# A hybrid attention stage on one core: heads alternate between two kinds, with five items of lead instead of three

## The reference, cut to what matters

```python
def sb_attend(q_pos, q, k, v, k_pos):
    z = einsum('bhqd,bhkd->bhqk', q, k) * (HEAD_DIM ** -0.5)
    mask = k_pos[None, :] < q_pos[:, None]
    log_skip = where(mask, log_sigmoid(-z), 0.0)
    later = cumsum(log_skip, axis=3, reverse=True) - log_skip
    w = where(mask, exp(log_sigmoid(z) + later), 0.0)
    return einsum('bhqk,bhkd->bhqd', w, v)

def fox_attend(q_pos, q, fq, k, v, k_pos, fk):
    z = einsum('bhqd,bhkd->bhqk', q, k) * (HEAD_DIM ** -0.5)
    z = z + fq[..., :, None] - fk[..., None, :]
    z = where(k_pos[None, :] <= q_pos[:, None], z, -inf)
    return einsum('bhqk,bhkd->bhqd', softmax(z), v)
```

## Time and profile before

| what | value |
|---|---|
| median of 3 runs | 1671.12 us (1670.85 to 1672.43) |
| the profiled execution | 1671.85 us |
| its span in the profile | 1670.1 us |
| TensorE busy, share of the span | 1488.6 us, 89% |
| VectorE busy | 939.3 us, 56% |
| ScalarE busy | 755.8 us, 45% |
| mean granted TensorE clock | 0.951 |

### The profile page before, as it was taken

The page is one execution under the profiler, slowest core; times in us unless marked ns, Lnnn a source line. Parts: engine busy times, 40 slices in busy tenths (PEclk is TensorE's granted clock), DMA queues, the critical chain, the costliest instruction groups (busy, mean ns, idle before and its releaser), DMA issues. The chain is left out here.

```text
span 1670.1 us, 23300 instructions
## 1 busy us (share of the span) xinstructions
PE 1488.6 (89%) x8581; PEld 1318.0 (79%) x8581; DVE 939.3 (56%) x1189; ACT 755.8 (45%) x1079; POOL 181.5 (11%) x129
## 2 busy tenths in 40 slices
PE   5999999999999988888999989969955998999950
PEld 3689899999999977777899989958844876788840
DVE  7622012223324338888766635442246998999948
ACT  8622011223333327776666622131114876777823
POOL 0000000000000010000000001111103334334320
PEclk9999999999999989999999989979966999999975
DMA  8355444457666568575677433444316899999538
GB/s 294 91 154 184 131 133 140 149 166 220 197 208 206 186 178 206 156 187 128 148 176 180 103 102 123 155 166 142 116 50 218 254 337 291 277 280 280 102 52 325
DMA packets 233075, 300.10 MB, mean 180 GB/s; under 512 B 86441, under 2 KB 171537, under 8 KB 232954
## 3 DMA queue, kind: packets, MB, share of 16 engines
q1 hardware_dynamic: 223458, 264.01, 51.8%
q0 software_dynamic: 9504, 34.61, 8.7%
HBM read 264.23 MB, written 87.81 MB: 211 GB/s over the span
## 5 line engine op out<-in xcount | busy, mean ns | idle before, releaser
L745 PE MATMUL G<-hhi,proj_whi 128*128 128x384 f32 x768 | 178.7, 341 | 0.0
L745 PE MATMUL G<-hhi,proj_wlo 128*128 128x384 f32 x768 | 176.4, 338 | 0.0
L745 PE MATMUL G<-hlo,proj_whi 128*128 128x384 f32 x768 | 176.3, 338 | 0.0
L1995 DVE TENSOR_TENSOR experts_ulo<-plain,experts_uhi 128x2048 fp32r<-128x2048 f32 x66 | 151.1, 2290 | 16.6 <-ACT experts_uhi L1939 9.8
L1098 PE MATMUL G<-items_WT,items_vt 128*128 128x128 f32 x1152 | 151.7, 277 | 0.3 <-DMA items_vc<-in_cache_sb_v_dram 0.3
L1098 PEld LDWEIGHTS G<-items_WT,items_vt 128*128 128x128 f32 x1152 | 142.2, 192 | 1.1 <-DMA items_vc<-in_cache_sb_v_dram 0.5
L1939 ACT ACTIVATE experts_uhi<-plain 128x2048 fp32r x66 | 126.7, 1921 | 33.6 <-PEq L80 23.4
L745 PEld LDWEIGHTS G<-hhi,proj_whi 128*128 128x128 f32 x768 | 136.1, 188 | 2.7 <-DVE proj_wlo L825 2.2
L745 PEld LDWEIGHTS G<-hhi,proj_wlo 128*128 128x128 f32 x768 | 138.0, 188 | 0.0
L745 PEld LDWEIGHTS G<-hlo,proj_whi 128*128 128x128 f32 x768 | 137.9, 188 | 0.0
L1896 PE MATMUL G<-experts_uhi,experts_ghi 128*128 128x512 f32 x264 | 108.9, 412 | 8.3 <-DVE experts_glo L1999 7.0
(11 more groups left out here) (313 smaller groups left out, 3030.9 us busy)
## 6 DMA issues: line engine op xcount, KB each, us to landing
plain<-in_w_dram SPq DMA_DIRECT2D x132, 512.0 KB
plain<-in_w_dram SPq DMA_DIRECT2D x33, 1024.0 KB
proj_wraw<-in_w_ada_dram SPq DMA_DIRECT2D x32, 512.0 KB
proj_wraw<-in_w_in_dram SPq DMA_DIRECT2D x20, 512.0 KB
qkhi_d<-proj_ohi SPq DMA_DIRECT2D x16, 576.0 KB, 2.8
qklo_d<-proj_olo SPq DMA_DIRECT2D x16, 576.0 KB, 3.0
gate_d<-proj_full SPq DMA_DIRECT2D x16, 576.0 KB, 3.7
merge_sg<-gate_d SPq DMA_DIRECT2D x16, 576.0 KB, 6.4
```

Source lines behind the costliest of these rows:

```text
L745: m = pe.matmul(G[:, g + c, 0:CH], w[r][:, k, :], a[:, k, c * CH:(c + 1) * CH], start=k == 0 and q == 0, stop=k == KD - 1 and q == 2)
L1995: dve.tensor_tensor(half(ulo[j], c), raw_up(side[n], c), half(uhi[j], c).bitcast(F32), ALU.subtract).then_inc(u_lo, 1)
```

## The change

All of it is in stage_items:
- The heads alternate, SB head h and then FoX head h. q, k, kc, vt, vc and W2 have one buffer for each kind. F has one buffer (fb) instead of two.
- AHEAD becomes 5: six S buffers (with as many maxima and sums), four R buffers (RING). ScalarE's exponent and VectorE's stick and invert move to i+4, weigh, least and scores to i+5.
- The cached-key scores of a head are computed with item 1, in the bank that item 1 leaves free, and added up by VectorE (add_past) there; item 3's scores wait for this sum, and the late item transposes zt itself. turn_past goes.
- high_y copies y from PSUM into one of three buffers yt (y_taken), waits for this copy, and rounds from there into yhi. The y bank is free once the copy is made. low_y runs at i-4 (LATER) and reads yt instead of the bank.

```diff
-                AHEAD = 3
+                AHEAD = 5
+                RING = 4
-                fb = [sb(f"fb{j}", [P, SEQ + 2 * P]) for j in both]
+                fb = sb("fb", [P, SEQ + 2 * P])
-                R = [sb(f"R{i}", [P, SEQ]) for i in range(2)]
+                R = [sb(f"R{i}", [P, SEQ]) for i in range(RING)]
+                NY, LATER = 3, 4
+                yt = [sb(f"yt{i}", [P, 512]) for i in range(NY)]
-                heads = [(k // H, k % H) for k in range(2 * H)]
+                heads = [(k % 2, k // 2) for k in range(2 * H)]
...
                         if f:
-                            if h >= 2:
-                                sp.wait_ge(min_ready, TT * (h - 1))
-                            load_f(h)
-                        if k % 2 == 0 and k:
-                            if k >= 4:
-                                sp.wait_ge(pv_done, n_pv[TT * (k - 2)])
-                            load_v(k // 2)
+                            if h:
+                                sp.wait_ge(min_ready, TT * h)
...
+                        if h % 2 == 0 and k:
+                            if k >= 2:
+                                sp.wait_ge(pv_done, n_pv[TT * (k - 1)])
+                            load_v(f, h, u)
...
+                        if t == 1:
+                            pe.wait_ge(kc_in[f], KC_DMAS * (h + 1))
+                            for b in range(NB):
+                                new = slice(SEQ + b * NQ, SEQ + (b + 1) * NQ)
+                                m = pe.matmul(G[:, g + 1, b * 2 * NQ:(b + 1) * 2 * NQ], kc[f][:, b * PAST:(b + 1) * PAST], qs[f][:, :, new],
+                                              start=True, stop=True)
+                            m.then_inc(z_past, 1)
+                        if t == 3:
+                            pe.wait_ge(z_summed, n // TT + 1)
                         if t < TT - 1:
...
                         else:
...
+                            pe.transpose(G[:, g, 0:P], zt[:], ident[:])
+                            m = part(G[:, g, P:2 * P], ks[f][:, SEQ:T], mnew[f])
+                        m.then_inc(z_ready, 1)
-                    def turn_past(n):
-                        pe.wait_ge(z_summed, n // TT + 1)
-                        pe.transpose(G[:, slot(n), 0:P], zt[:], ident[:]).then_inc(z_ready, 1)
...
                         if t % 4 == 0 and y >= 2:
-                            pe.wait_ge(y_lo, y_done[y - 1])
+                            pe.wait_ge(y_taken, y_done[y - 1])
...
-                        if 0 <= i + AHEAD < NI and late(i + AHEAD):
-                            turn_past(i + AHEAD)
...
-                        if o >= 2:
-                            act.wait_ge(scanned, o - 1)
+                        if o >= RING:
+                            act.wait_ge(scanned, o - RING + 1)
...
                         act.wait_ge(pv_done, n_pv[n + 1])
+                        if y >= NY:
+                            act.wait_ge(y_lo, y_done[y - NY + 1])
+                        for a, _, w, first in parts:
+                            act.activation(stage[a, first:first + w], G[a, 4 + y % 2, first:first + w], ACT.Copy).then_inc(y_taken, 1)
+                        act.wait_ge(y_taken, y_done[y + 1])
+                        for a, t0, w, first in parts:
+                            act.activation(yhi[a, 4 * f + h // 2, t0:t0 + w], stage[a, first:first + w], ACT.Copy).then_inc(y_hi, 1)
...
-                        if 0 <= i + 2 < NI and items[i + 2][0] == 1:
-                            exponent(i + 2)
-                        if 0 <= i + 3 < NI and items[i + 3][0] == 0:
-                            weigh(i + 3)
+                        if 0 <= i + AHEAD - 1 < NI and items[i + AHEAD - 1][0] == 1:
+                            exponent(i + AHEAD - 1)
+                        if 0 <= i + AHEAD < NI and items[i + AHEAD][0] == 0:
+                            weigh(i + AHEAD)
...
-                    for i in range(-AHEAD, NI + 2):
-                        if 0 <= i + 3 < NI and late(i + 3):
-                            add_past(i + 3)
-                        if 0 <= i + 2 < NI and items[i + 2][0] == 0:
-                            stick(i + 2)
-                        if 0 <= i + 3 < NI and items[i + 3][0] == 1 and not late(i + 3):
-                            least(i + 3)
-                        if 0 <= i + 2 < NI and items[i + 2][0] == 1:
-                            invert(i + 2)
-                        if 0 <= i + 3 < NI and items[i + 3][0] == 1 and late(i + 3):
-                            least(i + 3)
-                        if 0 <= i - 2 < NI and y_last(i - 2):
-                            low_y(i - 2)
+                    for i in range(-AHEAD, NI + LATER):
+                        if 0 <= i + AHEAD < NI and items[i + AHEAD][2] == 1:
+                            add_past((i + AHEAD) // TT)
+                        if 0 <= i + AHEAD - 1 < NI and items[i + AHEAD - 1][0] == 0:
+                            stick(i + AHEAD - 1)
+                        if 0 <= i + AHEAD < NI and items[i + AHEAD][0] == 1:
+                            least(i + AHEAD)
+                        if 0 <= i + AHEAD - 1 < NI and items[i + AHEAD - 1][0] == 1:
+                            invert(i + AHEAD - 1)
+                        if 0 <= i - LATER < NI and y_last(i - LATER):
+                            low_y(i - LATER)
```

More of the change, by code:

```diff
@@ L920, in stage_items @@
                 v_in = [sem(f"v_in{f}") for f in both]
[L921 to L922 removed]
+                f_in, masks, z_past, z_first, z_summed = sem("f_in"), sem("masks"), sem("z_past"), sem("z_first"), sem("z_summed")
                 z_ready, s_ready, r_ready, scanned, sb_ready = sem("z_ready"), sem("s_ready"), sem("r_ready"), sem("scanned"), sem("sb_ready")
@@ L1034, in scores @@
                         f, h, t = items[n]
-                        g, side = slot(n), n // TT % 2
+                        g = slot(n)
                         if n == TT - 1 or n == TT:
@@ L1047, in part @@
                         def part(out, key, mask):
-                            pe.matmul(out, qs[side][:, 0, q], key, start=True, stop=False)
+                            pe.matmul(out, qs[f][:, 0, q], key, start=True, stop=False)
                             if mask is not None:
@@ L1051, in part @@
                                 pe.matmul(out[:, w - P:w], identb[:], mask[:], start=False, stop=False)
-                            return pe.matmul(out, qs[side][:, 1, q], key, start=False, stop=True)
+                            return pe.matmul(out, qs[f][:, 1, q], key, start=False, stop=True)
+                        if t == 1:
+                            pe.wait_ge(kc_in[f], KC_DMAS * (h + 1))
+                            for b in range(NB):
+                                new = slice(SEQ + b * NQ, SEQ + (b + 1) * NQ)
[4 more added lines that the diff above has]
+                            pe.wait_ge(z_summed, n // TT + 1)
                         if t < TT - 1:
@@ L1104, in values @@
                                 new = slice(b * NQ, (b + 1) * NQ)
-                                m = pe.matmul(pair[:, :, new], vc[v][:, b, :], W2[v][:, 0, :, new], start=False, stop=b == NB - 1)
+                                m = pe.matmul(pair[:, :, new], vc[f][:, b, :], W2[f][:, 0, :, new], start=False, stop=b == NB - 1)
                         m.then_inc(pv_done, 1)
@@ L1153, in high_y @@
                         f, h, t = items[n]
+                        y = y_use(n)
+                        stage = yt[y % NY]
+                        parts = [(slice(e * HD, (e + 1) * HD), t // 4 * 4 * P, (t % 4 + 1) * P, e * P if late(n) else 0) for e in (both if late(n) else (h % 2,))]
                         act.wait_ge(pv_done, n_pv[n + 1])
-                        for e in both if late(n) else (h % 2,):
-                            a, t0, w = slice(e * HD, (e + 1) * HD), t // 4 * 4, (t % 4 + 1) * P
-                            first = e * P if late(n) else 0
-                            act.activation(yhi[a, 4 * f + h // 2, t0 * P:t0 * P + w], G[a, 4 + y_use(n) % 2, first:first + w], ACT.Copy).then_inc(y_hi, 1)
+                        if y >= NY:
[5 more added lines that the diff above has]
+                            act.activation(yhi[a, 4 * f + h // 2, t0:t0 + w], stage[a, first:first + w], ACT.Copy).then_inc(y_hi, 1)
                     for i in range(-AHEAD, NI + 2):
```

79 lines of the change are left out of this document (33 added, 46 removed).

## The result

The changed kernel takes 1674.96 us (median of 8 runs, 1673.57 to 1677.18) against 1671.18 us before (8 runs): ratio 1.0030, interval 1.0021 to 1.0039. It is slower, by 0.3%; forecast were 1662.9 us and a range up to 1672.0. The profiled execution took 1674.44 us, its span is 1672.7 us.

What follows compares the result with a forecast made beforehand. SB heads were held to be bound by a TensorE-VectorE-ScalarE loop, FoX heads by TensorE. Gain -25.1, start +7.0, stalls +9.1 and end +0.8 make -8.2 us: 1662.9 us, range 1651.5 to 1672.0.

Steps and rivals of the forecast that it cites:

- ScalarE: nothing in the sum: Items stage: ScalarE's mean 18.1 us a head stays under TensorE's 20.24, so its extra copies and switches cost nothing.
- The stalls: SB heads: TensorE waits for VectorE's first minimum, 1.3 us each, +9.1 us for seven heads, ends 0 and 14.7.
- the 0.85 us "at worst": Behind VectorE's minimum: exponential, doubled y copy and next take delay item 7's transpose by some 0.85 us more at worst.
- -25.1 us as the gain: Items stage: every head runs at the FoX pace, eight head lengths falling from 187.0 to 161.9 us.
- -16.0: From the first head's mark to the last one's: the gain of -25.1 plus stalls of 9.1 us.
- Start and end: Stage start +7.0 us, as TensorE waits for cached keys until about 628; end +0.8 for one more y copy.
- Loads: Heads' transfers, with F in one buffer: same bytes, freed well ahead of need, so 0 us; ends 0 and 3.
- (b): Rival: loops on both VectorE and ScalarE bite, 2.1 us a head, 14.7 in all; 1668.5 us; chance 0.15.
- (c): Rival: ScalarE becomes the bound through 14 more function switches, 17.9 us on top of the forecast; 1680.8; chance 0.07.
- the pair (42.8, limit 43): Sign: two successive heads take 41.8 us; the forecast is wrong if outside 40.5 to 43.
- kc (628.7, limit 630): Sign at the start: cached keys land near 628 us; the forecast is wrong if after 630.
- The third: Sign: the forecast is wrong if transposes wait for ScalarE's take for more than 10 us in all.

Runs made afterwards that it cites:

- half a sigmoid: Changed kernel with ScalarE's second sigmoid over half of the keys and VectorE's product reading R instead: 1693.94 us, one execution.
- old order: Changed kernel with all 8 SB heads first, then all 8 FoX heads, buffers by turn and two F buffers: 1671.53 us, ratio 1.0002 to the kernel before.
- half a scan: Changed kernel with VectorE scanning only half of the keys: 1683.44 us, one execution.
- kc first: Changed kernel with SyncE issuing the first head's cached keys kc ahead of its v: 1673.79 us, ratio 1.0016 to the kernel before.
- y copies alone: Kernel before plus three yt buffers, ScalarE copying y then rounding, residual from yt at i-4; three items ahead: 1668.84 us, ratio 0.9987.
- lead alone: Kernel before with only five items of lead, six S and four R buffers: 1692.52 us, ratio 1.0138.
- the old order with the start mended: Changed kernel with SB heads before FoX heads, first kc loaded ahead of v, past scores at item 3: 1666.11 us, ratio 0.9976 to the kernel before.
- y rounded directly: Changed kernel with y treated as before: ScalarE rounds from PSUM, residual from PSUM two items later: 1688.9 us, ratio 1.0104 to the kernel before.
- no switch: Changed kernel with FoX's exponential replaced by a sigmoid of the same size, so ScalarE never switches function: 1675.61 us, ratio 1.0032 to the kernel before.

## Why the prediction was wrong

**The failed step is "ScalarE: nothing in the sum".** The forecast compared ScalarE's mean, 18.1 us a head, with TensorE's 20.24, and let the difference hide everything. Its total was about right: 83.08 of 100 and 65.29 of 80 busy are 17.8 and 17.5 us for a mean head of 21.4. But the y copies of the head before and an SB head's sigmoids of 768 to 1024 columns stand in one unbroken row, the takes between them are late, and TensorE waits: 2.9 us in two pairs of heads, of 3.7 in which it stands idle. The sum did not have this term at all. The timeline shows it; the waits fall to 2.0 us when GpSimd rounds and to 1.3 with half a sigmoid. The same waits stand in the SB heads of the old order.

**The stalls were put on another wait.** The forecast had 1.3 us a pair, on TensorE's wait for VectorE's first minimum. That wait occurs once, in the first FoX head (2.7 us); later TensorE reaches the score just as the minimum is done. Behind it the take is late by 0.4 us in every second pair; that is what became of the 0.85 us "at worst", named and then left to the range. VectorE's chain is still close: half a scan shortens B by 0.8 us, and a gain on ScalarE brought the wait for the minimum back (0.7 and 1.1 us in two pairs). So a pair lost 2.3 us instead of 1.3 and the seven pairs behind head 1 lost 16.5 instead of 9.1: 7.4 too many.

**Head 1** had no term, since the sum's seven stalls are those of the seven later pairs. It took 23.3 us against TensorE's 20.2, 3.0 us, 2.7 of them the wait for the minimum: VectorE had the scans of the first head still to do. An earlier kc does not shorten this wait (2.9 us with kc first).

**-25.1 us as the gain** was nearly right: by TensorE's marks the way from 328.0 us to 15 heads of 20.24 is 24.4, 0.7 less. The pace of the FoX heads can be had with all of the change, a FoX pair of the old order takes 40.6 us against 40.5; with the y copies alone and a lead of three it is 41.0. With 7.4 and 3.0 this 0.7 makes the 11.1 us between -16.0 and -4.9.

**Start and end:** +7.8 forecast, +8.4 measured; kc at 628.7 against 628.

**Loads** at nothing, with F in one buffer: right, no wait for q, F or v in the steady part. **The rivals:** (b), ScalarE and VectorE both in the loop with 2.1 us, is nearest to what happened in the pairs, with 2.3 measured; its total, 1668.5, missed for head 1 and for the part behind the stage. (c), slower by switches, had the sign and not the mechanism: 15 loads of 1283 ns, and their removal changes nothing. The Trainium skill ("ScalarE: Activation LUTs", "What ACT_TABLE_LOAD costs") adds a drain of about 1380 ns to each load. This trace does not show one: behind the seven loads of the sigmoid's table the next instruction starts 0.02 us later or sooner, and the eight of the exponential's are followed by ScalarE's wait for VectorE's minimum, as at 777.00.

Of the prediction's signs of being wrong, the pair (42.8, limit 43) and kc (628.7, limit 630) did not fire. The third did, just: over the stage TensorE's transposes wait 10.3 us for ScalarE's take, where 10 was the limit.

**Not forecast:** 2 us more before the merge's first product. The interval was 6.1 to 6.2 us in three kernels (before, lead alone, y copies alone) and 6.8 to 8.1 in the others; what sets it stays open.

The parts by themselves, against the kernel before: lead alone +1.4% (with a lower clock), y copies alone -0.1%, lead with past scores moved and y copies 0.0% (old order), the same with alternation +0.3%. The lead did not pay without the other two parts, and alternation takes back more than it gives: it trades SB pairs of 44.1 and FoX pairs of 40.6, mean 42.4, for a pair of 42.8.

## What to carry to other kernels

Balancing two kinds of work by their means holds only over a stretch that the buffers span: set each engine's longest unbroken row of work against what the bound engine has to do meanwhile, for every engine and every kind of border. A cost on an engine "with slack" goes into the sum when a copy that the bound engine waits for stands behind it in the same queue. When halving one engine's work moves a stall instead of removing it, two chains are tight, and relief has to come to both. What paid here was the old order with the start mended (-0.2%), and with it the rounding moved to the idle GpSimd (-0.4%). Read the granted clock of each stretch before a longer head is put down to a queue: with the lead alone the clock was worth about as much as the whole loss.

## What the runs showed of the hardware

**TensorE's clock can fall in the middle of the work.** In the runs above the granted clock fell to the lower level with or behind waits of 1.9 us (y rounded directly), 2.9 us (kc first, head 1) and 2.5 to 3.2 us (lead alone), and once each behind waits of 0.6 and 0.95 us (no switch, half a scan). It stayed at 1.00 behind one of 2.7 us (changed kernel, head 1), so the length of the wait alone does not decide it. After its pause of 6.9 us at the start TensorE worked from 628.7 us at a granted clock of 0.50 until 636, 7 us; before the change 1.00 was granted from 626 after work had begun at 621.3.

**GpSimd's casts of y lengthened VectorE's work where they met it.** A cast of 64x512 took 711 ns on average in the changed order and 739 in the old one. In the changed order it falls on VectorE's product of 768 columns (959 to 1155 ns, shown above). In the old order it falls on the scan of 768 columns (groups of VectorE, without and with the casts):

```profile
L1198 DVE TENSOR_TENSOR_SCAN items_SC<-items_R,items_zer 128x768 f32<-128x768 f32 x8 | 14.1, 1758 | 0.8
L1204 DVE TENSOR_TENSOR_SCAN items_SC<-items_R,items_zer 128x768 f32<-128x768 f32 x8 | 16.2, 2027 | 0.8
```

The seven scans that meet a cast took 1.98 to 2.19 us, the one that meets none 1.76. Scans of 896 and 1024 columns that a cast meets in part were not longer.
